# Memory's two projections taken from the start of a two-block transformer kernel to its last attention, and two norms in separate steps

## What is computed

```python
u = rmsnorm(h, norm_mix_g[l]); proj = u @ w_in[l]                    # first block, start
ob = rmsnorm(ob, gla_norm_g[l]); yb = (ob * silu(ob_gate)) @ w_proj_b[l]
q = (rmsnorm_2(c_q, g_cq) @ w_qb); kv = (rmsnorm_2(c_kv, g_ckv) @ w_kvb)   # second block, latents
mem_n = rmsnorm_2(mem, g_mem[l])
k = mem_n @ wk; v = mem_n @ wv                                       # each 256 x 512
x = x + softmax(q @ k.T * C_DIM**-0.5) @ v @ wo                      # four heads of 128
```

## Time and profile before

| | |
|---|---|
| runs of the kernel before | 2589.67, 2590.18, 2590.25 us |
| median | 2590.18 us |
| the profiled execution's own time | 2588.82 us |
| its span in the trace | 2586.9 us |
| PE busy | 2555.4 us (99% of the span), 12005 matmuls |
| DVE, ACT, POOL busy | 1408.9, 1190.0, 178.6 us |
| DMA | 480.21 MB, mean 186 GB/s |
| granted TensorE clock, mean | 0.998 |

### The profile page before, as it was taken

How to read it: one execution, slowest core, us unless ns; L and a number is a source line. 1 busy time by engine, 2 the same in 40 slices (tenths; PEclk the granted TensorE clock), 3 DMA queues, 4 the chain that set the end, 5 groups by cost and what they waited for, 6 DMA issues and landing times.

```text
span 2586.9 us, 32313 instructions
## 1 busy us (share of the span) xinstructions
PE 2555.4 (99%) x12005; PEld 2144.4 (83%) x12005; DVE 1408.9 (54%) x1609; ACT 1190.0 (46%) x1570; POOL 178.6 (7%) x184
## 2 busy tenths in 40 slices
...
GB/s 273 236 170 126 178 146 184 192 186 242 213 192 187 189 186 193 191 193 187 189 183 179 184 177 130 181 140 213 135 203 179 192 193 192 184 183 195 188 185 155
DMA packets 249253, 480.21 MB, mean 186 GB/s; under 512 B 15088, under 2 KB 33696, under 8 KB 247984
## 3 DMA queue, kind: packets, MB, share of 16 engines
...
...
## 4 chain that ended last, share of the span: by engine, by line
PE 96%; DVE 1%; ACT 1%; issue 1%; POOL 0%; DMA 0%; ACTq 0%; SPq 0%; POOLq 0%; DVEq 0%
PE acc L1262 90%; PE unit L1285 3%; PE psO L1416 1%; PE psS L1344 0%; PE psS L1388 0%; DVE w_lo L1534 0%; PE unit L1344 0%; ACT w_hi L1033 0%; POOL rtmp L892 0%; DMA mem_sb<-in_mem 0%; DVE gla L1781 0%; PE unit L1467 0%; POOL stat L880 0%; ACT p L1157 0%; DVE xT_lo L1539 0%
## 5 line engine op out<-in xcount | busy, mean ns | idle before, releaser
L1534 DVE TENSOR_TENSOR w_lo<-w_raw,w_hi 128x1024 fp32r<-128x1024 f32 (+4 forms) x892 | 1080.5, 1215 | 1012.4 <-ACT w_hi L1033 1007.5
L1033 ACT ACTIVATE w_hi<-w_raw 128x1024 fp32r<-128x1024 f32 (+4 forms) x892 | 925.1, 1041 | 1041.4 <-PE acc L1262 1025.0
L1262 PE MATMUL acc<-w_hi,xT_hi 128*128 128x512 f32 (+4 forms) x2432 | 943.8, 388 | 3.5 <-DVE w_lo L1534 3.5
L1262 PE MATMUL acc<-w_lo,xT_hi 128*128 128x512 f32 (+4 forms) x2432 | 933.0, 384 | 0.0
L1262 PE MATMUL acc<-w_hi,xT_lo 128*128 128x512 f32 (+4 forms) x2432 | 932.1, 383 | 0.0
L1262 PEld LDWEIGHTS acc<-w_hi,xT_hi 128*128 128x128 f32 x2432 | 457.2, 188 | 88.4 <-DVE w_lo L1534 4.2
L1262 PEld LDWEIGHTS acc<-w_lo,xT_hi 128*128 128x128 f32 x2432 | 456.8, 188 | 86.3
L1262 PEld LDWEIGHTS acc<-w_hi,xT_lo 128*128 128x128 f32 x2432 | 457.4, 188 | 82.8 <-issue 0.5
L1262 PE MATMUL acc<-w_hi,hT_hi 128*128 128x512 f32 x864 | 337.0, 390 | 0.0
L1262 PE MATMUL acc<-w_lo,hT_hi 128*128 128x512 f32 x864 | 336.2, 389 | 0.0
L1262 PE MATMUL acc<-w_hi,hT_lo 128*128 128x512 f32 x864 | 336.1, 389 | 0.0
...
## 6 DMA issues: line engine op xcount, KB each, us to landing
w_raw<-in_w_in SPq DMA_DIRECT2D x168, 512.0 KB, 3.6
w_raw<-in_w_up SPq DMA_DIRECT2D x128, 512.0 KB, 3.8
w_raw<-in_w_down SPq DMA_DIRECT2D x128, 512.0 KB, 3.7
w_raw<-in_w_ffn_gate SPq DMA_DIRECT2D x88, 512.0 KB, 3.8
w_raw<-in_w_ffn_up SPq DMA_DIRECT2D x88, 512.0 KB, 3.7
w_raw<-in_w_ffn_down SPq DMA_DIRECT2D x88, 512.0 KB, 3.7
w_raw<-in_w_out SPq DMA_DIRECT2D x64, 512.0 KB, 4.1
...
```

What stands on the lines that cost most here:

```text
L1033: act.activation(w_hi[:, slot, 0:kc, 0:n], w_raw[:, slot, 0:kc, 0:n], ACT.Copy).then_inc(hi_split, 1)
L1262: ins = pe.matmul(ac[t][:, 0:n], a[:, l0 + c, t * P:(t + 1) * P], w[:, slot, c, 0:n], start=start and c == 0 and m == 0, stop=stop and c = ...
L1534: dve.tensor_tensor(w_lo[:, slot, 0:kc, 0:n], w_raw[:, slot, 0:kc, 0:n], w_hi[:, slot, 0:kc, 0:n].bitcast(F32), ALU.subtract).then_inc(lo_ ...
```

## The change

It moves and regroups steps; no dense product is added or taken away. First, memory's load, turns and two projections go from the start to the second half of the last mixing product and to the cross attention: `load_mem` steps behind tiles 3 to 6 of `into_norm(5, ...)`, one unit of `mem` behind each of the tiles 8 to 15 (counted from 1), k in front of the query block, v behind it. k and v stay on chip, so the store and reload fall away. Second, x itself is turned at the start (mode "gain", with the gain turned by PE as for `mem`), so POOL's 8 multiplications and their broadcast load fall away, and the first tile is two parts. Third, the norm of GLA's heads is made per token half in three slots (squares, root, norm), with POOL multiplying `obg` by the norm's gain ahead of it (`gla_gain`) in place of a multiplication behind it; `c_norm` is split into `c_root` and `c_norm`; `angles` goes to the first FFN; `bias_row` goes into the second block. Fourth, in the cross attention outputs alternate between `psO` and `psS`, and probabilities have four buffers.

```diff
-    S += [("gain_T",)]
-    T = lambda j, t: ("T", f"mem{j}", t)
-    S += [T(0, 0), ("lead",), T(0, 1), ("lead",)]
-    between = [[T(1, 0), T(1, 1), ("lead",)], [T(2, 0)], [T(2, 1)], [T(3, 0), ("ssq", 0, 0, 0), ("ssq", 0, 0, 1)],
-               [T(3, 1), ("ssq", 0, 1, 0), ("ssq", 0, 1, 1)], [("ssq", 0, 2, 0), ("ssq", 0, 2, 1)],
-               [("ssq", 0, 3, 0), ("ssq", 0, 3, 1), ("rstd", 0, 0), ("rstd", 0, 1)]]
-    mem_dense = block_steps("w_k_cross_2", 0, DC, 0, 512, "memT", 0, "ckv", 0, ("mem0", "mem1", "mem2", "mem3"))
-    mem_dense += block_steps("w_v_cross_2", 0, DC, 0, 512, "memT", 0, "ckv", 1)
-    xu = [(j, t) for j in range(4) for t in range(NT)]
-    squares = [[("ssq", 1, j, t)] for j, t in xu]
-    xs = between + [[("gained", 1, j, t) for j, t in xu]] + squares[:1]
-    xs += [[("T", f"u{j}", t)] + s for (j, t), s in zip(xu, squares[1:] + [[("rstd", 1, 0), ("rstd", 1, 1)]])]
-    S += weave(mem_dense, xs, 1)
-    S += [("keep_ckv",), ("bias_row",), ("half_rms",)]
     w = lambda c0, n, evac, arg=0, needs=(): block_steps("w_in", 0, DC, c0, n, "xT", 0, evac, arg, needs)
-    S += w(0, 512, "qkva", 0, U_NEEDS) + w(512, 512, "qkva", 512) + w(1024, 512, "qkva", 1024)
+    T = lambda j, t: ("T", f"x{j}", t)
+    ssq = lambda n, j: [("ssq", n, j, t) for t in range(NT)]
+    roots = lambda n: [("rstd", n, t) for t in range(NT)]
+    first = w(0, 512, "qkva", 0, ("x0", "x1", "x2", "x3"))
+    S += [("gain_T", "x"), T(0, 0), ("lead",), T(0, 1), ("lead",)]
+    S += [("part", first[0][1], 0, 0), ("part", first[0][1], 0, 1), T(1, 0), T(1, 1), ("lead",), ("lead",)]
+    S += weave(first[1:], [[T(2, 0), ("gain_T", "mem")], [T(2, 1)], [T(3, 0)] + ssq(1, 0), [T(3, 1)] + ssq(1, 1),
+                           ssq(1, 2), ssq(1, 3) + roots(1)], 1)
+    S += [("half_rms",)]
...
-    slots += [[("gla_att", t)] for t in range(NT)]
-    slots += [[("gla_out", t, h)] for t in range(NT) for h in (0, 2)]
-    slots += [[("gla_norm",)], [], both("ya0"), both("ya1"), both("yb0"), both("yb1")]
+    slots += [[("gla_att", t), ("gla_gain", t)] for t in range(NT)]
+    slots += [[("gla_out", 0, 0)], [("gla_out", 0, 2)], [("gla_squares", 0), ("gla_out", 1, 0)], [("gla_root", 0), ("gla_out", 1, 2)]]
+    slots += [[("gla_norm", 0), ("gla_squares", 1)], [("gla_root", 1)], [("gla_norm", 1)]]
+    slots += [both("ya0"), both("ya1"), both("yb0"), both("yb1")]
...
-    S += [("gain", 3), ("gain", 4)] + up(0) + [("swiglu_up", 0, 6)] + both("glu6") + [("down", "w_ffn_down", 0, 24)]
+    S += [("gain", 3), ("gain", 4)] + weave(up(0), [[], [("angles",)]], 1) + [("swiglu_up", 0, 6)] + both("glu6") + [("down", "w_ffn_down", 0, 24)]
...
-    S += weave(dense, [[], [("c_norm",)], [("angles",)], [("rope", "kr")], both("cq"), both("ckv"), both("kr")], 2)
+    S += weave(dense, [[("c_root",)], [("c_norm",)], [("key_zeros",), ("rope", "kr")], [], both("cq"), both("ckv"), both("kr")], 2)
...
-    S += into_norm(5, [make_block("w_out_2", 8, 8, 512 * j, 512, "xT", 8, "add", 512 * j, () if j else ("s0", "s1"))
-                       for j in range(4)], {(2, 1): 0, (2, 3): 1, (3, 2): 2})
-
-    q = make_block("w_q_cross_2", 0, DC, 0, 512, "xT", 0, "cqo", 0, U_NEEDS)
-    S += out_of_norm(5, q, whole=5)
-    S += both("ck") + [("gain", 6)]
+    steps = into_norm(5, [make_block("w_out_2", 8, 8, 512 * j, 512, "xT", 8, "add", 512 * j, () if j else ("s0", "s1"))
+                          for j in range(4)], {(2, 1): 0, (2, 3): 1, (3, 2): 2})
+    turned = [[("T", f"mem{j}", t)] for j in range(4) for t in range(NT)]
+    S += weave(steps, [[], [], [("load_mem", 0)], [("load_mem", 1)], [("load_mem", 2)], [("load_mem", 3)], []] + turned, 1)
+    k = block_steps("w_k_cross_2", 0, DC, 0, 512, "memT", 0, "ckv", 0, ("mem0", "mem1", "mem2", "mem3"))
+    S += weave(k, [roots(5), both("u3"), ssq(0, 0), ssq(0, 1), ssq(0, 2), ssq(0, 3) + roots(0)], 1)
+    S += weave(block_steps("w_q_cross_2", 0, DC, 0, 512, "xT", 0, "cqo", 0, U_NEEDS), [[], both("ck"), [("gain", 6)]], 1)
     g = GROUP0["C"]
-    S += [("part", q, k, 0) for k in range(5, 8)] + [("evac", q, (0,)), ("part", q, 5, 1), ("T", "cqq", 0), ("lead",)]
-    S += [("part", q, 6, 1), ("scores", g), ("part", q, 7, 1), ("evac", q, (1,)), ("scores", g + 1), ("T", "cqq", 1)]
-    S += [("probs_T", g), ("scores", g + 2), ("output", g), ("probs_T", g + 1), ("scores", g + 3)]
-    S += [("output", g + 1), ("lead",), ("probs_T", g + 2), ("T", "co", 0), ("lead",), ("output", g + 2),
-          ("probs_T", g + 3)]
+    S += weave(block_steps("w_v_cross_2", 0, DC, 0, 512, "memT", 0, "ckv", 1),
+               [[("T", "cqq", 0)], [("T", "cqq", 1)], [("scores", g)], [("scores", g + 1)], [("probs_T", g), ("scores", g + 2)],
+                [("probs_T", g + 1), ("scores", g + 3)], [("probs_T", g + 2)]], 1)
+    S += [("probs_T", g + 3), ("output", g), ("output", g + 1), ("output", g + 2), ("T", "co", 0), ("lead",), ("output", g + 3)]
     o = make_block("w_o_cross_2", 0, 4, 0, 512, "coT", 0, "add", 0, ("co",))
-    S += [("part", o, 0, 0), ("output", g + 3), ("part", o, 1, 0), ("T", "co", 1), ("part", o, 0, 1), ("part", o, 1, 1)]
-    S += [("lead",), ("lead",), ("evac", o, (0, 1))] + pieces_of_norm(6, 0)
+    S += [("part", o, 0, 0), ("T", "co", 1), ("part", o, 1, 0), ("lead",), ("part", o, 0, 1), ("part", o, 1, 1)]
+    S += [("evac", o, (0, 1))] + pieces_of_norm(6, 0)
     blocks = [None] + [make_block("w_o_cross_2", 0, 4, 512 * j, 512, "coT", 0, "add", 512 * j) for j in (1, 2, 3)]
     S += into_norm(6, blocks, {(2, 0): 0, (3, 0): 1, (3, 1): 2})
 
...
-            return s2, p2, pT2, scale, 128
+            return s2, p2, pT4 if kind == "C" else pT2, scale, 128
+
+        def slot(kind, g):
+            return g % (4 if kind == "C" else 2)
+
+        def out_bank(kind, g):
+            return psS if kind == "C" and g % 2 else psO
 
         def values(kind, kt, h):
...
                                      t_in[s[1]][row:row + 2 * P, bass.ds(r * 1024 + j * 512, 512)], 2, 512)
+                elif s[0] == "load_mem":
+                    j = s[1]
+                    c = slice(512 * j, 512 * j + 512)
+                    sp.wait_ge(unit_done, LAST_UNIT["s1", 1] + 1)
+                    sp.dma_start(mem_sb[:, :, c], tok(t_in["mem_2"][0])[:, :, c]).then_inc(mem_in[j], 16)
...
-                elif s[0] == "gla_norm":
-                    rstd(50, 8)
-                    for t in range(NT):
-                        pool.wait_ge(ob_normed, t + 1)
-                        v = gla[:, t, 0:1024]
-                        pool.tensor_tensor(v, v, obg[:, t, :], ALU.mult).then_inc(ob_ready, 1)
+                elif s[0] == "gla_gain":
+
+                    t = s[1]
+                    for arg in (0, 384, 704):
+                        block_read(pool, BLOCK["obg", arg], t)
+                    v = obg[:, t, :].rearrange("p (h v) -> p h v", h=G_HEADS)
+                    pool.tensor_tensor(v, v, glag[:].unsqueeze(1).broadcast_to([P, G_HEADS, G_VAL]), ALU.mult).then_inc(obg_gained, 1)
+                elif s[0] == "gla_root":
+                    rstd(50 + G_HEADS * s[1], G_HEADS)
                 elif s[0] == "evac" and s[1]["evac"] == "merge":
                     j = s[1]["arg"] // 512
...
                     units_read(pe, LAST_UNIT["probs", g])
-                    if g:
+                    if kind == "C":
+                        pe.wait_ge(out_done, max(GROUP0["C"], g - 1))
+                        pe.wait_ge(sc_read, GROUP0["C"] + NGROUPS["C"])
+                        if g == GROUP0["C"]:
+                            for tt in range(NT):
+                                block_read(pe, BLOCK["ckv", 1], tt)
+                    elif g:
...
                     dve.tensor_copy(gla[:, s[1], 512:1024], bank[U % 2][:]).then_inc(unit_free[U % 2], 1)
+                elif s[0] == "gla_root":
+                    t = s[1]
+                    dve.wait_ge(head_squares, G_HEADS * (t + 1))
+                    mean(50 + G_HEADS * t, G_HEADS, G_VAL, by=4.0)
                 elif s[0] == "gla_norm":
-                    dve.wait_ge(head_squares, 8)
-                    rstd(at["root"], 50, 8, G_VAL, by=4.0)
-                    for t in range(NT):
-
-                        c = 50 + G_HEADS * t
-                        after(dve.tensor_scalar(stat[:, c:c + G_HEADS], stat[:, c:c + G_HEADS], over_rms(1, t), None, ALU.mult))
-                        for h in range(G_HEADS):
-                            v = gla[:, t, G_VAL * h:G_VAL * (h + 1)]
-                            c = 50 + 4 * t + h
-                            ins = dve.scalar_tensor_tensor(out=v, in0=v, scalar=stat[:, c:c + 1], in1=glag[:],
-                                                           op0=ALU.mult, op1=ALU.mult)
-                        ins.then_inc(ob_normed, 1)
+                    t = s[1]
+                    c = 50 + G_HEADS * t
+                    dve.wait_ge(rstd_ready, GLA_ROOT[t] + 1)
+                    dve.wait_ge(obg_gained, t + 1)
```

(21 more changed lines are left out.)

137 lines of the change are left out of this document (62 added, 75 removed).

## The result

The changed kernel takes 2613.55 us (median of 4 runs, 2610.52 to 2616.06); the kernel before took 2590.22 beside it. The ratio is 1.009 [1.0078, 1.0102]: slower by 23.3 us, where I forecast 2589.3 us, 0.9 faster. The four runs lie in two groups, 2610.5 and 2611.1 us at a mean granted clock of 0.998, and 2616.1 us twice at 0.997; the profiled one is of the first group. The profiled execution's span is 2609.3 us, 22.4 more than before.

A forecast was written before the change was run, and what follows sets the result against it. The prediction took PE, busy 99% of the span, as the bound, so only its idle time could move. Won 9.7 us less lost 8.8 made it 0.9 faster: 2589.3 us for the median, range 2582.5 to 2594.0.

The forecast's parts named there:

- The step that failed: Whole kernel: with no dense product removed and small instructions nearly unchanged, only PE's idle time can move.
- start, idle: Kernel start: first tile starts 1.9 us earlier, less a new wait before the third tile; 0.7 us won.
- `bias_row`: At 64.68 us: its 0.97 us wait as third unit in a row goes in its new place; 1.0 us won.
- GLA's norm: GLA's heads: 2.5 us of PE idle time and a 1.7 us clock fall go; 4.2 us won.
- latents, angles: Wait for `w_lo` behind `c_norm` and the angle chain goes, the chain moving to the first FFN; 1.0 us won.
- cross attention, idle: Cross attention: v's tiles cover scores, softmax and probabilities; idle falls from 4.8 to 2.0 us, 2.8 won.
- memory's turns, idle: Last mixing product: a unit of `mem` before two of u makes PE wait for banks at three places; 8.0 us lost.
- clock: Last mixing product: PE's idle time may lower its clock; half of one 1.7 us fall, 0.8 us lost.
- the first place: End of the mixing product's second block: `mem`'s unit ahead of the block's adds delays u's units, 3.8 us lost.
- One wait for v's copy, about 0.3: Cross attention, after v's last tile: PE waits about 0.3 us for v's copy, putting the first output at 0.8.
- SP's wait: First `load_mem`: SP stands about 7 us for the sparse attention's last turn, but no weight comes late; nothing lost.
- the case that I gave 0.08: Rival: POOL and DVE collide at both block ends of the last mixing product, 1.27 us each: 2591.8 us; chance 0.08.

The follow-up runs named there:

- e1: Changed kernel with the new 64-byte gain_T_mem table moved into the unused half of `unwanted`, restoring the later buffers' old addresses; 2592.43 us, ratio to before 1.0008.
- e2: Kernel before the change with 64 empty bytes ahead of x_sb and nothing else; 2610.29 us, ratio to before 1.0082.
- e11: e1 with squares, root and norm of GLA's norm back in one slot, POOL's product by the gain still ahead; 2592.56 us, ratio to before 1.0007.
- e10: e1 with v's last tile in two parts and v's copy directly behind each, ahead of the lead; 2590.25 us, ratio to before 1.0003.

## Why the prediction was wrong

**The step that failed** is in the first paragraph: "The change takes no dense product away, and the count of PE's small instructions stays the same but for one turn of a gain. So it can only move idle time of PE." A change can also alter what each matmul costs, by where its operands lie. This one did so for 3408 of them, and 21.1 of the 23.3 us are that (e1, e2). The sum put this term at nothing without a reason, no rival held it, and the range ended at 2594.0. The line was in the diff that I worked from; I read it as a buffer without a price. The range would have held e1, at 2592.4, but that doesn't prove the rest of the sum: the forecast was 0.9 us faster, and e1 is 2.5 slower than before (not clear of noise), by errors that partly cancel.

**The other steps**, against e1's profile (for the idle time the changed kernel's is the same within 0.3):

| step | predicted | measured in e1 |
|---|---|---|
| start, idle | -0.7 | -0.4 (idle in the first 20 us 8.8, now 8.4) |
| `bias_row` | -1.0 | -1.0 |
| GLA's norm | -4.2 | -4.2 (nothing of it is left) |
| latents, angles | -1.0 | -1.0 (the two waits for `w_lo` that are left are the start's) |
| cross attention, idle | -2.8 | -0.8 |
| memory's turns, idle | +8.0 | +7.0 |
| clock | +0.8 | +3.4 in the mixing product, +1.7 in the cross attention |
| sum | -0.9 | +4.7 (the span grew by 4.8) |

This is the profiled execution, with three falls of the clock. The median of e1's runs is 2.5 us above before.

- The start: the first product came at 9.78 in the changed kernel (9.4 predicted), and the wait before the third tile is 0.94 (0.8 to 0.9 predicted). But the next pair of units came at 14.62, where I had 14.0, and the third tile at 19.94, no earlier than before (19.83). I let the first tile take as long as before; it took 4.8 us in place of 4.4. PE's first products start 0.43 us apart in both kernels, although the granted clock is given as 1.00, until 13.8 now and 14.4 before, so a tile that starts earlier has more of them at that rate. Little of the 0.7 was won:

```profile
9.78 0.77 PE L1258 MATMUL acc<-w_hi,xT_hi 128*128 128x512 f32 x1 [1.44 <-DVE w_lo L1538]
10.34 0.63 PE L1258 MATMUL acc<-w_hi,xT_lo 128*128 128x512 f32 x1
10.77 0.63 PE L1258 MATMUL acc<-w_lo,xT_hi 128*128 128x512 f32 x1
...
14.62 1.04 PE L1281 MATMUL unit<-cst,x_sb 128*128 128x128 f32 x8
...
19.94 0.47 PE L1258 MATMUL acc<-w_hi,xT_hi 128*128 128x512 f32 x1 [0.94 <-DVE w_lo L1538]
```

- GLA's size was right and half of its reason wrong. POOL's product beside DVE's was named, and that is 2.1 us of it. But I gave "With the steps two tiles apart none of these waits stays on DVE", and e11 shows that their distance didn't matter. Of the 4.2, 1.7 are a fall of the clock, and that part is luck of the execution: e2 has the same wait (2.56 us) and no fall behind it.
- Memory's turns were right in mechanism and place, and 1.0 too high in size: 1.50 and 1.51 us at the first place, where I had 3.8 together, then 2.02 and 2.02 for 2.1 and 2.1. These rows are of the changed kernel:

```profile
1737.55 0.66 PE L1281 MATMUL unit<-cst,u 128*128 128x128 f32 x4 [1.50 <-DVE memT_lo L1638]
1739.72 0.65 PE L1281 MATMUL unit<-cst,u 128*128 128x128 f32 x4 [1.51 <-DVE memT_lo L1638]
...
1749.21 0.66 PE L1281 MATMUL unit<-cst,u 128*128 128x128 f32 x4 [2.02 <-DVE memT_lo L1638]
...
1761.89 0.66 PE L1281 MATMUL unit<-cst,u 128*128 128x128 f32 x4 [2.02 <-DVE memT_lo L1638]
```

- The cross attention's term was mis-sized in one number: "One wait for v's copy, about 0.3". It was 2.7 to 2.9. A lead stands ahead of the copy on ACT and DVE, which I had not counted; but with the copy ahead of the lead (e10) 1.5 us are left, so the copy itself was priced too low as well.
- The clock: the changed kernel's profile shows no fall in the mixing product and one in the cross attention, e1's shows two and one, for the same idle times; e1's runs spread from 2588.6 to 2593.6, about what three falls of 1.7 make. So "half of one fall" was a guess about something that differs between executions; the price of one was right (5 x 0.34 in e1 as in the earlier trace rows).
- SP's wait was as told: 7.8 us at the first load of `mem` (about 7 predicted), and no weight's DMA ended a wait of PE.

```profile
SPq L844 <- PE unit L1281: 7.8, 1, 7.8
```

- POOL and DVE did not collide at the ends of the mixing product's blocks, the case that I gave 0.08: from 1700 to 1800 us no lead of DVE in the changed kernel took over 1.26 us.
